# Hybrid attention block: the probabilities turned on VectorE and moved by DMA in place of TensorE transposes, the scores two iterations earlier

## What is computed

```python
h = rms_norm(x, norm_w)
q, k, v, g_a, u_p, g_p = split(h @ w_in, 6)          # w_in: 2048 x 6144
q, k = rope(rms_norm(q)), rope(rms_norm(k))           # 8 heads x 2 components x 64
p = softmax(q k^T / 8)                                # per head and component, 512 x 512
a = p[component 0] - lam * p[component 1]
o = rms_norm(a @ v, subln_w) * 0.8
pool = (centred_mean(u_p, windows 2, 4, 8, 16) - u_p) @ w_pool * pool_scale
out = x + concat(o * silu(g_a), pool * silu(g_p)) @ w_out
```

## Time and profile before

| | us |
|---|---|
| median of the runs | 780.72 |
| the profiled execution | 781.05 |
| its span, first to last instruction | 779.2 |
| TensorE (PE) busy | 771.3 (99%) |
| VectorE (DVE) busy | 551.8 (71%) |
| ScalarE (ACT) busy | 381.5 (49%) |
| GpSimd (POOL) busy | 31.3 (4%) |
| mean granted TensorE clock | 0.999 of full speed |

### The profile page before, as it was taken

One profiled execution on the slowest core, in us unless ns is written; L12 is line 12 of the kernel. 1 busy time (PEld: TensorE's weight loads), 2 busy tenths in 40 slices (PEclk: granted clock), 3 DMA queues, 4 the chain that ended last, 5 costly groups with the idle time before them and its releaser, 6 DMA issues.

```text
span 779.2 us, 9636 instructions
## 1 busy us (share of the span) xinstructions
PE 771.3 (99%) x3458; PEld 636.9 (82%) x3458; DVE 551.8 (71%) x861; ACT 381.5 (49%) x649; POOL 31.3 (4%) x42
## 2 busy tenths in 40 slices
PE   9999999999999999999999999999999999999997
PEld 8788888888888888888888888888888788888886
DVE  5543235887874787786478788448868969987796
ACT  5463234444374344446354436554445775655552
POOL 0010000000000000000000000000000003322200
PEclk9999999999999999999999999999999999999999
DMA  9853233452121354222244321224522169999962
GB/s 333 328 190 98 91 96 94 135 163 77 59 82 55 109 148 142 66 76 66 71 125 137 117 82 54 82 88 134 155 83 81 55 234 252 276 276 260 212 164 108
DMA packets 67079, 106.22 MB, mean 136 GB/s; under 512 B 5344, under 2 KB 46560, under 8 KB 66528
## 3 DMA queue, kind: packets, MB, share of 16 engines
q1 hardware_dynamic: 60288, 86.72, 34.2%
q0 software_dynamic: 4736, 16.78, 11.0%
q10 hardware_dynamic: 2016, 2.18, 0.9%
HBM read 95.17 MB, written 4.19 MB: 128 GB/s over the span
## 4 chain that ended last, share of the span: by engine, by line
PE 88%; DVE 3%; DMA 3%; ACT 3%; SPq 2%; issue 1%; DVEq 0%; ACTq 0%
PE ps L457 86%; PE ps L584 2%; DMA raw<-in_w_in 1%; DMA raw<-in_w_out 1%; SPq L329 1%; ACT probs L806 1%; SPq L286 1%; DVE w_lo L903 1%; DVE probs L1045 0%; ACT diff L814 0%; DVE diff L1093 0%; DVE wp_lo L1096 0%; DVE probs L1043 0%; DVE row_max L1062 0%; SPq L293 0%
## 5 line engine op out<-in xcount | busy, mean ns | idle before, releaser
L903 DVE TENSOR_TENSOR w_lo<-raw,w_hi 128x512 fp32r<-128x512 f32 x240 | 163.3, 689 | 165.7 <-ACT w_hi L685 90.1
L457 PE MATMUL ps<-h_hi,w_hi 128*128 128x512 f32 x640 | 250.9, 392 | 0.0
L457 PE MATMUL ps<-h_lo,w_hi 128*128 128x512 f32 x640 | 249.3, 390 | 0.0
L457 PE MATMUL ps<-h_hi,w_lo 128*128 128x512 f32 x640 | 171.1, 389 | 0.0
L685 ACT CAST w_hi<-raw 128x512 fp32r<-128x512 f32 x149 | 90.5, 620 | 159.8 <-PE ps L457 159.0
L457 PEld LDWEIGHTS ps<-h_hi,w_lo 128*128 128x128 f32 x640 | 120.1, 188 | 25.0
L457 PEld LDWEIGHTS ps<-h_hi,w_hi 128*128 128x128 f32 x640 | 120.2, 188 | 24.6
L457 PEld LDWEIGHTS ps<-h_lo,w_hi 128*128 128x128 f32 x640 | 120.2, 188 | 24.4
L457 PE MATMUL ps<-w_hi,h_hi 128*128 128x512 f32 x352 | 122.2, 391 | 1.7 <-ACT w_hi L675 1.3
L457 PE MATMUL ps<-w_lo,h_hi 128*128 128x512 f32 x352 | 121.4, 389 | 0.0
L457 PE MATMUL ps<-w_hi,h_lo 128*128 128x512 f32 x352 | 121.4, 389 | 0.0
(11 more groups left out here) (143 smaller groups left out, 785.7 us busy)
## 6 DMA issues: line engine op xcount, KB each, us to landing
raw<-in_w_in SPq DMA_DIRECT2D x96, 512.0 KB, 3.6
raw<-in_w_out SPq DMA_DIRECT2D x12, 512.0 KB, 3.8
raw<-in_w_out POOLq DMA_DIRECT2D x12, 512.0 KB, 17.1
wide_b<-in_w_out POOLq DMA_DIRECT2D x12, 512.0 KB, 18.4
x_rows<-in_x SPq DMA_DIRECT2D x4, 1024.0 KB, 13.0
tall<-in_w_out SPq DMA_DIRECT2D x8, 512.0 KB, 13.5
tall<-in_w_out POOLq DMA_DIRECT2D x8, 512.0 KB, 23.4
mixed<-in_x_cols SPq DMA_DIRECT2D x3, 1024.0 KB, 13.2
```

The source lines that it names most:

```text
L457: last = nc.tensor.matmul(dst, lhs, rhs, start=first and i == 0, stop=final and i == len(pairs) - 1, skip_group_check=True)
L903: nc.vector.tensor_tensor(w_lo[:, slot, :], src, w_hi[:, slot, :].bitcast(F32), ALU.subtract).then_inc(w_lo_ready, 1)
```

## The change

- The transposes on TensorE are gone. VectorE now transposes the joined probabilities of an item in 32x32 blocks (one instruction, reading every fourth element) into a buffer `turned`, and SyncE moves them to their partitions with four transfers of 64 KB an item (`move_item`) into `at_raw`. ScalarE's copy to `at_hi` and VectorE's subtraction for `at_lo` now read SBUF. The matmuls with V read the keys in pieces of 32 (`key_tile`). There are six slots for items instead of four.
- Scores are at m = 22+2i, maxima at 23+2i, exponentials at 24+2i, the joining and the new transpose at 25+2i; the copy to `at_hi` stays at 28+2i, but now stands behind the exponentials of item i+2, and the subtraction stays at 28+2i.
- The column groups of a round come in the order Q, U, GA, GP, K instead of Q, GA, U, GP, K. The chain of centred means is spread over m = 26 to 36.
- First stage: x and the first weights come in smaller first pieces, one of them on ScalarE's queue; the twelve small transfers of constants are issued later; the row of epsilons is spread by DMA and GpSimd instead of by a matmul; there are 9 warming matmul calls instead of 16.

```diff
-    Q, GA, U, GP, K = range(5)
-    COLUMNS = (0, 3 * A, 4 * A, 5 * A, A)
+    Q, U, GA, GP, K = range(5)
+    COLUMNS = (0, 4 * A, 3 * A, 5 * A, A)
...
+        def item_place(i):
+            return (i, i) if i < ST else ((i + 2 - ST) % ST, (i + 2 - ST) % ST + 2)
...
-            load_x_cols(0, 0, 2)
-            load_v(0)
-            load_x_cols(1, 2, 4)
+            load_x_cols(0, 0, 1)
+            load_x_cols(1, 1, 2)
+            sp.dma_start(raw[:, 0, 512:1024], w_in_rows[:, 1, V_COLUMN:V_COLUMN + NC]).then_inc(raw_in[0], 16)
+            load_x_cols(2, 2, 4)
             load_v(1)
...
+            def move_item(rnd, i):
+                slot = item_place(i)[1]
+                sp.wait_ge(at_turned, rnd * ITEMS + i + 1)
+                for a in range(ST):
+                    sp.dma_start(at_raw[:, slot, a * P:(a + 1) * P],
+                                 turned[32 * a:32 * a + 32, slot, :]).then_inc(at_moved[i % 2], 16)
...
+                    if unit >= 10 and unit - 10 < ITEMS:
+                        move_item(r, unit - 10)
...
-                    i, odd = divmod(m - 24, 2)
+                    i, odd = divmod(m - 22, 2)
...
-                        for t in range(ST):
-                            last = nc.tensor.transpose(ps[:, TB, t * P:(t + 1) * P],
-                                                       probs[:, 0, t * P:(t + 1) * P], ident[:, :])
-                        last.then_inc(at_transposed, 1)
...
-                if v == 24:
-                    pe.wait_ge(eps_diag_ready, ST)
-                    pe.wait_ge(v_lo_ready, ST)
-                    nc.tensor.matmul(ps[:, 0, :], ones_f32, eps_diag, start=True, stop=True).then_inc(eps_spread, 1)
...
+            act.dma_start(raw[:, 0, 0:512], w_in_rows[:, 0, V_COLUMN:V_COLUMN + NC]).then_inc(first_half_in, 16)
...
+                    i, odd = divmod(m - 24, 2)
+                    if 0 <= i < ITEMS and not odd:
+
+                        act.wait_ge(max_ready, r * ITEMS + i + 1)
+                        if i:
+                            act.wait_ge(at_turned, r * ITEMS + i)
+                        for c in range(2):
+                            nc.scalar.activation(probs[:, c, :], ps[:, S0 + c, :], ACT.Exp,
+                                                 bias=neg_max[:, c:c + 1], scale=SCALE,
+                                                 accum_out=row_sum[:, c:c + 1]).then_inc(exp_done, 1)
+                    if 2 <= i < ITEMS + 2 and not odd:
+
+                        slot = item_place(i - 2)[1]
+                        act.wait_ge(at_moved[i % 2], r * (ITEMS // 2 * ST * 16) + ((i - 2) // 2 + 1) * ST * 16)
+                        nc.scalar.copy(at_hi[:, slot, :], at_raw[:, slot, :]).then_inc(at_hi_ready, 1)
...
-                    i, odd = divmod(m - 25, 2)
+                    i, odd = divmod(m - 23, 2)
...
-                        nc.vector.scalar_tensor_tensor(out=probs[:, 0, :], in0=probs[:, 1, :],
-                                                       scalar=coef[:, :], in1=probs[:, 0, :],
-                                                       op0=ALU.mult, op1=ALU.add).then_inc(attn_ready, 1)
+                        chain(nc.vector.scalar_tensor_tensor(out=probs[:, 0, :], in0=probs[:, 1, :],
+                                                             scalar=coef[:, :], in1=probs[:, 0, :],
+                                                             op0=ALU.mult, op1=ALU.add))
+                        if i - 1 == ST + 2:
+                            dve.wait_ge(head_done, r * 2 + 1)
+                        nc.vector.transpose(
+                            turned[:, item_place(i - 1)[1], :].rearrange("p (c t i) -> p c t i", c=4, t=ST),
+                            probs[:, 0, :].rearrange("p (t j c) -> p c t j", t=ST, c=4)).then_inc(at_turned, 1)
...
-WARM = 16
+WARM = 9
```

223 lines of the change are left out of this document (110 added, 113 removed).

## The result

The changed kernel takes 814.35 us, median of 812.04 to 815.78, where the kernel before takes 781.62 beside it. The ratio is 1.041, interval 1.038 to 1.044. So it is 32.7 us slower, where I forecast 11.3 and a range that ended at 808. The profiled execution took 813.38 us.

A forecast was written before the change was run, and what follows sets the result against it. TensorE was taken as the bound, busy 771.3 of 779.2 us. From the profiled 781.05, removing 20.2 gives 760.8; adding 31.5 of waits in the loop gives 792.3, forecast as 792 us, range 777 to 808, with 786 to 800 at 0.50.

The forecast's parts named there:

- The loop: From one item's exponentials to the next: 8.31 us in series against TensorE's 6.37; waits of 7.9 us a round, 31.5 in four.
- the recurrence: Item-by-item times in the second round, when each item's exponentials end against when TensorE is due, giving its waits.
- the list of signs: What the new profile should show, including scores waiting at items 1, 3, 4 and 5 by 2.2, 1.4, 1.9 and 1.9 us.
- So it costs 0.41 to 1.24 us in the order, and I take 0.66: Price of the new transpose in VectorE's order, taken from the shuffle of the same tile form: 0.66 us.
- Behind item 7 TensorE has the pool product and the second head, and VectorE catches up: After a round's last item TensorE has other work, so no further wait was counted there.
- What is removed: TensorE spared 14.4 us of transposes, 0.9 epsilon matmul, 1.9 waits at transposes, the first-stage wait 1.3, and 1.7 at the start: 20.2.
- Q moved in time: Scores two iterations earlier find Q moved; its second transfer would have to land by 292.14.
- The transfers hidden: An item's four transfers take 6 us; item 0 has 9.7, so they lie hidden with 3.7 us to spare.
- U ahead of GA free, epsilons free: Column order's cost is already in the loop; spreading epsilons on GpSimd has tens of us of room.
- The matmuls with V: Reading keys in pieces of 32 costs nothing unless they stream slower: 96 matmuls, up to 22 us at twice the time.
- The slow transpose: Rival: VectorE's transpose, reading every fourth element, costs 1.24 us; waits 11.4 us a round, time 806; chance 0.17.
- The short loop: Rival: VectorE's order between maxima at m = 28 to 34 is short enough; 777 with copy and low part hidden; chance 0.15.

The follow-up runs named there:

- the order mended and the step left in: Changed kernel with copy ahead of exponentials, evacuation ahead of item 7's joining, maximum ahead of split, second head's Q low parts behind first maximum: 783.89 us.
- the three ways around the step: Keys reordered outside the transpose: in K's casts (813.77 us) or score matmuls (809.69), against the changed kernel; in exponentials' output, with four order edits added (788.53).

## Why the prediction was wrong in size

The sum was made against the profiled execution, and so is the account: forecast 792.3, found 813.4, 21.1 us apart.

- **The loop (forecast 31.5, found 40.4).** The mechanism and every place were right: the copy behind the exponentials, VectorE's low part waiting for it, the first maximum late. S0 to S7 sums to 229.7 in four rounds against 189.3 without waits. By the recurrence the waits stand ahead of the scores of items 1, 4, 5 and 6, and there they are; "items 1, 3, 4 and 5" in the list of signs is a slip. The step that failed is "So it costs 0.41 to 1.24 us in the order, and I take 0.66". It is 1.03. The prediction's own recurrence with 1.03 in place of 0.66 gives waits of 2.2 at item 1, 2.3 at items 4, 5 and 6 and 0.7 at item 7, which is 10.1 a round and 40.4 in four. The measured pairs exceed 6.37 by 2.2, 2.2, 2.1 and 2.2 in the first round, at the same places. That the sums agree to the digit is luck: the rounds have 9.4, 12.2, 10.7 and 8.1, and some 4 us of that is TensorE at half clock behind items 1 and 6, of which 2.3 us are then missing from the evacuation's wait. With the transpose at 0.63 in the order, as it is without its step, the 0.66 of the prediction would have stood.
- **"Behind item 7 TensorE has the pool product and the second head, and VectorE catches up" (forecast 0, found 8.1).** Group K writes the bank that the evacuation at m = 40 reads, and on VectorE that stands behind the joining, the transpose and the split of item 7. I followed the loop to its last score and not to VectorE's next duty with a reader. The run with the evacuation first shows it, and the run with the copy first shows that it is the chain's tail.
- **What is removed (forecast 20.2, found 18).** A round without waits is 3.6 us shorter, 14.4 in four, where 14.4 and 1.9 stood in the sum: the waits that the weight loads had at the transposes cost TensorE hardly any time. The first scores come at 157.57 in place of 166.50; without the two iterations (5.45) that is 3.5 us for the start, the wait and the epsilons, forecast 3.9. It holds for a start at the full rate; in the run with the copy first, which starts at the slow one (last section), they come at 159.76. The first real matmul starts near 6.0, not 5.4.
- **Q moved in time** held but for one wait of 0.9 us. K to S0 is 1.3 us over its shortest in all.
- **The transfers hidden, U ahead of GA free, epsilons free**: no wait of TensorE names them, and the run that makes the transfers twice agrees on the first. No run takes the other two back, nor puts the scores back to m = 24 by itself.
- **The matmuls with V**: the 12 of a head take 2.84 us from start to start for 2.72 before, so pieces of 32 keys cost 0.12 us a head, 1 in all, of the 22 left open.
- **The clock**, on which the prediction is silent, fell in seven places, of which two cost something: some 3 us.
- **The rivals.** The slow transpose was nearer the truth than my choice: 1.03 us in the order, against its 1.24 and my 0.66. Its time of 806 lacked the evacuation. The short loop with the copy and the low part hidden was priced at 777 with the cheap transpose; the run that hides them takes 786.4 with the dear one, and exceeds the sum without waits by 5.6 us a round between S0 and S7 for 4.0. The rule of the Trainium skill (VectorE: DVE Perf Modes, section "Rules for kernel authors"), to transpose 128x128 on TensorE, holds here: no order that I found gets the change below the kernel before.

Where the gain of 18 us went is shown for the most part. The copy's place and its tail take 28, in which the 3 us of the clock are. The step of the transpose takes 11 to 13, which overlaps with it. With the order mended and the step left in, 3 us of loss stay; the three ways around the step that keep the output cost as much as they gave, or more. What holds the stretch then is VectorE's amount of work: 7.0 to 8.2 us a pair with no wait in its rows where TensorE's pair is 6.37, and pairs that shrink with the work. How the last 3 us divide between it and the start isn't shown. No version beat the kernel before, and keeping its transposes with the new start (up to 3.5 us of gain) was not tried.

## What to carry to other kernels

When work moves off the bound engine, lay out the whole cycle of the engines that take it, each instruction between two of its turns, and follow it to the last thing that the bound engine reads from it, not only to the end of the loop. Put what waits for another engine (a copy, a cast) where the wait is covered: one instruction's place was worth 28 us here, more than the whole removal. And price an operation that reads with a step apart from its plain form.

## What the runs showed of the hardware

- A step of four float32 (16 bytes) costs on three engines, not equally: VectorE's transpose 1.10 us for 0.71, VectorE's subtraction of 64x512 1.07 us where twice the elements took 1.22, ScalarE's cast of 64x512 1.11 us where twice the elements took 1.05, a matmul of 512 columns 0.46 us for 0.23. ScalarE writing with a step of 128 bytes: 1.20 us for 0.68. Matmuls that read pieces of 32 elements hardly notice: 2.84 us for 2.72, for twelve.
- The first matmuls run at either rate in otherwise like kernels. The windows of the kernel after and of the one with the copy first, 7 to 10 us:

```profile
7.00:10.00 3.00, 3.00 (x15) 2.49 (x14) 2.14 (x4) 2.00 (x4) 0.00 (x0) 1.00 1.05 406
```

```profile
7.00:10.00 3.00, 3.00 (x8) 2.32 (x8) 1.95 (x4) 1.81 (x4) 0.00 (x0) 1.00 1.05 407
```

15 matmuls against 8, and the first scores come 2.2 us apart (157.57 and 159.76), while the column of the granted clock says 1.00 for both. What decides it was not tried; by its size it can be a good part of the spread from run to run, which isn't shown.
